# A latent-token backbone on one core: the down products of three stages as seven half products instead of eight

## The chip, the cores and the metric

The kernel runs on one core of a Trainium2 chip. The metric is the device time of one execution in microseconds (us): the median of several runs. Beside the runs one execution was profiled; its trace is what the rows below are from. The engines are TensorE (PE, with its weight loads as PEld), VectorE (DVE), ScalarE (ACT), GpSimd (POOL) and SyncE (SP, which here only issues DMAs). Each takes its instructions in order; they wait for each other by semaphores.

## What is computed

The program is a two-layer backbone on 1024 tokens of width 1024 (float32), with 256 context tokens. Layer 0 has a mixer of neighbourhood attention and a recurrent group, then a SwiGLU FFN; layer 1 has a short gated convolution, then a SwiGLU FFN. The change lies in the last three of these four parts:

```
def swiglu(h, w_gu, w_down):
    gt, up = jnp.split(h @ w_gu, 2, axis=-1)
    return (jax.nn.silu(gt) * up) @ w_down

def short_conv_mixer(h, w_in, w_conv, w_out):
    bg, cg, xv = jnp.split(h @ w_in, 3, axis=-1)
    return (bg * dwconv(cg * xv, w_conv, SC_PAD)) @ w_out

# layer 0:  h = h + g1 * mixer(...);  h = h + g2 * swiglu(modulate(rmsnorm(h)), ...)
# layer 1:  h = h + g1 * short_conv_mixer(...);  h = h + g2 * swiglu(...)
# output:   rmsnorm(h, final_g)
```

The hidden width of the FFN is 2816 (22 tiles of 128), of the short convolution 1024 (8 tiles). The gates, shifts and scales (g1, g2, ...) are the mod vectors, the product of a conditioning vector with mod_w, 6 x 1024 per layer.

## The kernel before

Features lie on the 128 partitions, tokens on the free axis; h is 8 tiles of 128 x 1024 in SBUF. Every product is done in three matmuls on a high and a low part of each operand: w_hi x_hi, w_lo x_hi, w_hi x_lo (the helper product, lines 1099 to 1104, so all matmuls have the lines L1102 to L1104). The high part is a cast by ScalarE, the low part a subtraction by GpSimd or VectorE.

The last three parts are three stages, F0 (FFN of layer 0), S (short convolution), F1 (FFN of layer 1). Each has a first phase of pairs and a down phase.

A pair makes two feature tiles of the input projection for all tokens (gate and up of the FFN; in S two of three are "sum" pairs, which make cg and xv and then the taps of the convolution, and every third is a "gated" pair, which makes bg for two tiles). A pair is 7 half products instead of 8, by Winograd's form of Strassen's scheme: the token axis and the contraction are halved, sums of the quadrants of weights and tokens are multiplied, and sums of the products give the result. So each pair has four weight sums by VectorE (weight_sum, L2086), seven operands cast by ScalarE (operand_high, L1602) and subtracted by GpSimd (operand_low, L1054), and VectorE's sums of products (pair_sums, L2240), 84 matmuls in all. The operands of pair p+1 are made while pair p is multiplied. The gated result z, two halves of 512 tokens, is stored to DRAM (store_z, L776, from silu_g or conv_t). F0 and F1 have 22 pairs, S has 12. The first four pairs of a stage have their products 0 and 3 done ahead, in first_products (L1418).

The down phase multiplies z with w_down (w_out in S) in rounds of two hidden tiles: 11, 4 and 11 rounds. A round loads two z tiles and two weight tiles (load_round, L838; 512 KB each), ScalarE casts (down_high, L1656), GpSimd makes the low parts (down_low, L1070), and PE runs 16 groups, 8 feature tiles by 2 token halves, each of 6 matmuls (down_group, L1484). After each group VectorE adds gate x result to h (update, L2052). The last two rounds are taken together, so that each group is done once with 12 matmuls, and the norm of the next stage begins beside its second half. Three sets of operand tiles (a, b, c) rotate.

In F0's down phase VectorE also makes the mod vectors of layer 1: 48 units, each a load of 512 KB (load_mod_f, L787) and a multiply-add of 1024 elements (mod_unit, L2060), summed over partitions by PE every 8 units. At the end of F1 the 8 token tiles of h are transposed by PE, squared, scaled and stored, four of them beside the last groups (fin_products, L1533).

The order is written out by hand on each engine. SP issues nearly all loads and stores in one queue, in program order; a wait of SP holds back every later transfer. In a pair its order is: store the first half of z, load one weight tile for the next pair, store the second half, load the other (products_loads, L792 to L825).

## Time and profile before

| | us |
|---|---|
| median of 3 runs | 2291.04 |
| lowest, highest run | 2290.49, 2293.44 |
| profiled execution, its span | 2288.6 |
| TensorE busy | 2234.8 |
| VectorE busy | 1484.0 |
| GpSimd busy | 1143.8 |
| ScalarE busy | 840.3 |

The page gives the profiled execution's span alone, from its first to its last instruction; the runs lie some us above it for what lies around the program. Matmuls overlap in the trace (each lasts 390 ns or so and the next starts earlier), so the busy time of PE tells that it is working, and the distance of starts tells what one costs. The granted clock is at its full level (0.9 or more in each slice).

### The profile page before, as it was taken

The numbers are of one execution on the slowest core, as the hardware profiler recorded it, in microseconds if no ns is written. First come the engines' busy times: TensorE is split into PE (matmuls) and PEld (weight loads), VectorE is DVE, ScalarE is ACT, GpSimd is POOL, SyncE is SP. The second block draws the span as 40 slices with busy tenths as digits, with TensorE's granted clock in tenths as the row PEclk, the third lists the DMA queues.
The fourth block names the chain that finished last, engine by engine and source line by source line (L and its number), as shares of the span: only waits on it lengthen the run. The fifth ranks groups of instructions, "written<-read, shape, count | busy, mean of one in ns | idle before, by whom it ended". The sixth has DMA issues, their size and how long they took to land.

```text
span 2288.6 us, 27308 instructions
## 1 busy us (share of the span) xinstructions
PE 2234.8 (98%) x10246; PEld 1822.6 (80%) x10246; DVE 1484.0 (65%) x1897; ACT 840.3 (37%) x1396; POOL 1143.8 (50%) x726
## 2 busy tenths in 40 slices
PE   8999999999899999999999999999899999999998
PEld 3788887878688888888888778888688888888886
DVE  5677856854876555558777987665965555555553
ACT  4555546853523332331213522233533333332212
POOL 3323304788455555565434345574365555564340
PEclk9999999999999999999999999999999999999999
DMA  9756568734132222257662122260132222242321
GB/s 332 223 159 175 159 177 205 163 131 134 42 101 83 83 83 83 83 192 258 207 208 78 51 74 74 74 215 2 60 102 90 83 83 83 84 151 90 111 83 74
DMA packets 296942, 282.95 MB, mean 124 GB/s; under 512 B 64783, under 2 KB 242155, under 8 KB 296299
## 3 DMA queue, kind: packets, MB, share of 16 engines
q1 hardware_dynamic: 258747, 257.61, 36.4%
q10 hardware_dynamic: 37488, 21.50, 3.3%
q0 software_dynamic: 576, 2.10, 0.2%
q8 instruction: 82, 1.34, 0.2%
q14 instruction: 49, 0.40, 0.1%
HBM read 226.36 MB, written 57.16 MB: 124 GB/s over the span
## 4 chain that ended last, share of the span: by engine, by line
PE 85%; DVE 6%; DMA 2%; ACT 2%; issue 2%; POOL 1%; SPq 0%; ACTq 0%; DVEq 0%; POOLq 0%
PE bank L1102 27%; PE bank L1104 26%; PE bank L1103 26%; PE bank L1191 1%; DMA q_spill<-qk_raw 1%; PE bank L1332 1%; DVE act_lo L2138 1%; DVE act_hi L2138 1%; PE bank L1357 1%; PE bank L1145 1%; PE bank L1316 1%; PE bank L1358 0%; DVE probs L2519 0%; DVE x_rms L2130 0%; DMA k_lo<-k_spill 0%
## 5 line engine op out<-in xcount | busy, mean ns | idle before, releaser
L2057 DVE SCALAR_TENSOR_TENSOR h<-bank,mods,h 128x512 f32<-128x512 f32 x384 | 287.4, 750 | 260.4 <-PE bank L1104 255.3
L1063 POOL TENSOR_TENSOR slot_lo<-pair_raw,slot_hi 128x512 fp32r<-128x512 f32 x112 | 169.8, 1516 | 288.0 <-ACT slot_hi L1621 288.0
L1063 POOL TENSOR_TENSOR slot_lo<-t_sum,slot_hi 128x512 fp32r<-128x512 f32 x109 | 164.5, 1531 | 153.4 <-ACT slot_hi L1621 153.4
L1063 POOL TENSOR_TENSOR slot<-pair_raw,slot 128x512 fp32r<-128x512 f32 x144 | 232.2, 1634 | 16.0 <-ACT slot L1621 16.0
L2218 DVE TENSOR_TENSOR bank<-bank,p 128x512 f32<-128x512 f32 x53 | 37.0, 698 | 288.3 <-PE bank L1104 288.2
L1102 PE MATMUL bank<-act_lo,slot_hi 128*128 128x512 f32 x436 | 171.1, 392 | 6.6 <-DVE act_lo L2138 5.9
L1621 ACT CAST slot_hi<-pair_raw 128x512 fp32r<-128x512 f32 x112 | 69.0, 616 | 294.4 <-DMA pair_raw<-in_ffn_w_gu 243.6
L1102 PE MATMUL bank<-a,slot_hi 128*128 128x512 f32 x436 | 171.5, 393 | 2.8 <-ACT p L1630 0.9
L1104 PE MATMUL bank<-a,slot_hi 128*128 128x512 f32 x436 | 170.5, 391 | 0.0
L1103 PE MATMUL bank<-act_lo,slot_lo 128*128 128x512 f32 x436 | 169.9, 390 | 0.0
L1104 PE MATMUL bank<-act_lo,slot_hi 128*128 128x512 f32 x436 | 169.9, 390 | 0.0
L1103 PE MATMUL bank<-a,slot_lo 128*128 128x512 f32 x436 | 169.7, 389 | 0.0
L1102 PE MATMUL bank<-act_hi,w_hi 128*128 128x512 f32 x368 | 146.7, 399 | 3.3 <-DVE proj_lo L2392 2.7
L1103 PE MATMUL bank<-act_hi,w_lo 128*128 128x512 f32 x376 | 148.0, 394 | 0.0
L1074 POOL TENSOR_TENSOR act_lo<-low_f,act_lo 128x512 fp32r<-128x512 f32 x80 | 102.3, 1315 | 85.3 <-ACT act_lo L1661 85.3
L1103 PE MATMUL bank<-act_hi,slot 128*128 128x512 f32 x364 | 141.9, 390 | 0.0
L1104 PE MATMUL bank<-act_hi,slot 128*128 128x512 f32 x364 | 141.8, 390 | 0.0
L1102 PE MATMUL bank<-act_hi,slot 128*128 128x512 f32 x364 | 141.7, 389 | 0.0
L1621 ACT CAST slot_hi<-t_sum 128x512 fp32r<-128x512 f32 x109 | 67.8, 622 | 160.6 <-PE bank L1104 103.3
L1102 PE MATMUL bank<-act_lo 128*128 128x512 f32 x320 | 125.8, 393 | 0.0
L1104 PE MATMUL bank<-act_lo 128*128 128x512 f32 x320 | 125.1, 391 | 0.0
L1103 PE MATMUL bank<-act_lo 128*128 128x512 f32 x320 | 124.6, 389 | 0.0
(329 smaller groups left out, 5975.0 us busy)
## 6 DMA issues: line engine op xcount, KB each, us to landing
pair_raw<-in_ffn_w_gu SPq DMA_DIRECT2D x88, 512.0 KB, 4.6
mod_in_f<-in_mod_w SPq DMA_DIRECT2D x48, 512.0 KB, 3.7
z_spill<-silu_g SPq DMA_DIRECT2D x88, 256.0 KB, 2.6
mod_in_p<-in_mod_w SPq DMA_DIRECT2D x32, 512.0 KB, 4.5
pair_raw<-in_o_w_in SPq DMA_DIRECT2D x24, 512.0 KB, 3.8
raw<-in_e_w_in SPq DMA_DIRECT2D x20, 512.0 KB, 4.4
low_f<-z_spill SPq DMA_DIRECT2D x40, 256.0 KB, 5.1
a_f<-z_spill SPq DMA_DIRECT2D x18, 512.0 KB, 6.2
```

Source lines behind the costliest of these rows:

```text
L1063: nc.gpsimd.tensor_tensor(low, from_, high, ALU.subtract).then_inc(s_wlo, 1)
L1074: nc.gpsimd.tensor_tensor(lo, full, hi, ALU.subtract).then_inc(s_l2, 1)
L1102: pe.matmul(dst, w_hi, x_hi, start=first, stop=False)
L1103: pe.matmul(dst, w_lo, x_hi, start=False, stop=False)
L1104: return pe.matmul(dst, w_hi, x_lo, start=False, stop=last)
L1145: mm = pe.matmul(bank[:, b, m:m + 1], acc[:, m * P:(m + 1) * P], ones[:, 0:1], start=True, stop=True)
L1191: mm = pe.matmul(bank[0:2, 4 + 2 * c + a, :], cond[:, k, :], mod_ring[:, u % 8, a * HALF:(a + 1) * HALF], start=(k == 0), stop=(k == FT - 1))
L1316: pe.matmul(out_, q, kh[:, part], start=True, stop=False)
L1621: nc.scalar.copy(slot(st, n, p)[0], from_).then_inc(s_whi, 1)
L2057: V.scalar_tensor_tensor(out=dst, in0=bank[:, b, :], scalar=mods[:, gate, m:m + 1], in1=dst, op0=ALU.mult, op1=ALU.add).then_inc(s_hup, 1)
L2138: V.tensor_tensor(lo, LOW_F[n][k], hi, ALU.subtract).then_inc(s_ld, 1)
L2218: V.tensor_tensor(to, bank[:, x_bank(p), :], p1_at(p), ALU.add).then_inc(s_made, 1)
```

## The change

The down phase is now done by the same scheme as the pairs. For hidden tiles 2r and 2r+1 the weights are quartered (two tiles by two halves of the output features) and z likewise (two tiles by two token halves). Seven products, each over all pairs kp of hidden tiles, are accumulated in PSUM one after the other: a product of 11 (or 4) steps, a step being one 128 x 512 weight piece by one 128 x 512 token piece, 4 output tiles of 3 matmuls. DOWN gives for each product its weight operand, its token operand, the four banks, and whether the banks start fresh or go on; UPDATES gives the quadrants of h to which VectorE adds the banks when the product is complete. So some products pass into several quadrants of h, and a bank that is carried on serves the next product too. The last four steps of a stage are done output tile by output tile.

The token sums T1 to T4 are made by VectorE in the pairs, from the two z tiles in one buffer zt (z_sum), and stored beside B11, B21, B22: 7 pieces per pair of tiles. The weight sums S1 to S4 are made in the pairs too: SP loads the four quarters of two weight tiles (load_w) a pair ahead, GpSimd makes S1 and S3, VectorE S2 and S4, in place, and SP stores the four sums (store_w), which stand behind the next pair's loads in the queue. The working space for this, and for the mod units, is that of h: h is stored to DRAM in pair 1 of each stage (put_h_aside) and fetched back in the last but one (bring_h_back). The mod units move from F0's down phase into the pairs 4 to 19 of F0 (32 units) and 2 to 9 of S (16), two per pair, with their sum in SBUF where it was in PSUM; two buffers instead of four.

The down phase loads each step into one of 8 slots (load_step); ScalarE casts both pieces, GpSimd makes the low part of the weights, VectorE that of the tokens from the fifth step on. Norm, first operands and first half of the next stage are spread over the steps of the last products (down_step on ACT, DVE and POOL). In the final rows the upper features of tiles 4 to 7 are transposed and multiplied by the gain beside the last product, and the last rows are done by halves.

The core of the diff:

```
+B11, B21, B22, T1, T2, T3, T4 = range(7)
+S1, S3, S2, S4 = range(4)
+DOWN = (((0, 0), B11, XS, True), (S2, T2, YS, True), ((1, 0), B21, XS, False), (S3, T3, YS, False),
+        ((1, 1), T4, YS, False), (S1, T1, XS, True), (S4, B22, XS, False))
+UPDATES = (((0, 1), (1, 0), (1, 1)), ((0, 1),), ((0, 0),), ((1, 1),), ((1, 0),), ((1, 1),), ((0, 1),))
...
+def w_ops(st, p):
+    return [k for k in range(4 * KP[st]) if W_PAIR + k // 8 * 3 + k % 8 // 3 == p]
...
+def w_loads(st, p):
+    return [kp for kp in range(KP[st]) if W_PAIR + kp // 2 * 3 + kp % 2 - 1 == p]
...
+    def store_t(kp, c):
+        sp.wait_ge(*z_summed(kp, c))
+        store_z(c, kp, {T1: zt[:, 0, one], T2: p1[:, 1, :], T3: zt[:, 0, two], T4: zt[:, 1, one]}[c])
+    def store_w(st, k):
+        r, c = divmod(k, 4)
+        kp = KP0[st] + r
+        sp.wait_ge(*w_made(kp, c))
+        sp.dma_start(w_sums[c, r], w_part[:, kp % 2, W_PIECE[c], :]).then_inc(s_wst[kp % 2], 16)
+    def load_w(st, r):
+        kp = KP0[st] + r
+        if kp >= 2:
+            sp.wait_ge(s_wst[kp % 2], 64 * (kp // 2))
+        sp.wait_ge(s_hst, X_DONE + 16 * (st + 1))
+        for a in (0, 1):
+            for j in (0, 1):
+                sp.dma_start(w_part[:, kp % 2, 2 * a + j, :],
+                             weights_down(st)[(2 * r + j) * P:(2 * r + j + 1) * P, a * HALF:(a + 1) * HALF]).then_inc(s_wld[kp % 2], 16)
+    def put_h_aside(st):
+        sp.wait_ge(s_scal, 8 * (NORM[st] + 1 - N_F0) + FT)
+        sp.dma_start(h_spill, h[:, :, :]).then_inc(s_hst, 16)
+    def bring_h_back(st):
+        for j in (0, 1):
+            sp.wait_ge(s_wst[j], 64 * ((KP0[st] + KP[st] + 1 - j) // 2))
+        if st != F1:
+            sp.wait_ge(s_mfin, LT + (4 if st == F0 else MODS) + 1)
+        sp.dma_start(h[:, :, :], h_spill).then_inc(s_hld, 16)
+    def aside_work(st, p):
+        for k in w_ops(st, p):
+            store_w(st, k)
+        for r in w_loads(st, p):
+            load_w(st, r)
+        for u in mod_units(st, p + 1):
+            load_mod_f(u)
+        if p == PAIRS[st] - 2:
+            bring_h_back(st)
...
+    def load_step(st, i):
+        q, r = divmod(i, KP[st])
+        w, c, *_ = DOWN[q]
+        kp = KP0[st] + r
+        if i < RING:
+            sp.wait_ge(s_prod, product_at(st, (1, 1, 2, 2, 4, 5, 6, 6)[i], PAIRS[st] - 1) + 1)
         else:
+            sp.wait_ge(*step_done(st, i - RING))
+        landed = down_landed(st, i)[0]
+        if isinstance(w, tuple):
+            from_ = weights_down(st)[(2 * r + w[0]) * P:(2 * r + w[0] + 1) * P, w[1] * HALF:(w[1] + 1) * HALF]
+        else:
+            from_ = w_sums[w, r]
+        sp.dma_start(down_operand(i)[0][2], from_).then_inc(landed, 16)
+        sp.wait_ge(*stored(c, kp + 1))
+        sp.dma_start(down_operand(i)[1][2], z_parts[c, r]).then_inc(landed, 16)
...
+    def w_sum(st, k):
+        r, c = divmod(k, 4)
+        kp = KP0[st] + r
+        a11_, a12_, a21_, a22_ = (w_part[:, kp % 2, j, :] for j in range(4))
+        if c == S1:
+            pool.wait_ge(s_wld[kp % 2], 64 * (kp // 2 + 1))
+            ins = nc.gpsimd.tensor_tensor(a22_, a21_, a22_, ALU.add)
+        else:
+            ins = nc.gpsimd.tensor_tensor(a21_, a11_, a21_, ALU.subtract)
+        ins.then_inc(s_wsum, 1)
...
+    def bank_free(st, q, m):
+        if q == 0:
+            if m == 0:
+                pe.wait_ge(s_xfree, PAIR0[st] + PAIRS[st])
+            if m == 3 and st != F1:
+                pe.wait_ge(s_mset, LT + (4 if st == F0 else MODS))
+        elif q == 1:
+            if m == 0:
+                pe.wait_ge(*made(PAIR0[st] + PAIRS[st] - 1, C21))
+        else:
+            pe.wait_ge(*updated(st, {2: 0, 3: 1, 4: 3, 5: 2, 6: 5}[q], m))
+    def down_part(st, i, m):
+        q, r = divmod(i, KP[st])
+        banks, fresh = DOWN[q][2:]
+        if r == 0:
+            bank_free(st, q, m)
+        w, x = down_operand(i)
+        at_ = slice(m * P, (m + 1) * P)
+        end = r == KP[st] - 1
+        mm = product(bank[:, banks[m], :], (w[0][:, at_], w[1][:, at_]), x[0], x[1], fresh and r == 0, end, not fresh)
+        if end:
+            mm.then_inc(s_out, 1)
+        return mm
...
     def down_products(st):
+        for i in range(n - TAIL):
+            down_ready(st, i)
+            for m in range(4):
+                mm = down_part(st, i, m)
+            if i % KP[st] < KP[st] - 1:
+                mm.then_inc(s_step, 1)
+            down_joint(st, i)
+        for i in range(n - TAIL, n):
+            down_ready(st, i)
+        for m in range(4):
+            if st == F1 and m == 3:
+                fin_lower(4, (0, 1))
+                fin_lower(5, (0, 1))
+            for i in range(n - TAIL, n):
+                down_part(st, i, m)
...
+    def z_sum(kp, c):
+        a, b, c_, d, t2 = zt[:, 0, one], zt[:, 0, two], zt[:, 1, one], zt[:, 1, two], p1[:, 1, :]
+        if c == T1:
+            dve.wait_ge(*stored(B11, kp + 1))
+            ins = V.tensor_tensor(a, b, a, ALU.subtract)
+        elif c == T3:
+            dve.wait_ge(*z_summed(kp, T1))
+            ins = V.tensor_tensor(b, d, b, ALU.subtract)
+        elif c == T2:
+            if kp:
+                dve.wait_ge(*stored(T2, kp))
+            ins = V.tensor_tensor(t2, d, a, ALU.subtract)
+        else:
+            dve.wait_ge(*stored(B21, kp + 1))
+            dve.wait_ge(*z_summed(kp, T2))
+            ins = V.tensor_tensor(c_, c_, t2, ALU.subtract)
+        ins.then_inc(s_zsum, 1)
+    def w_sum(st, k):
+        r, c = divmod(k, 4)
+        kp = KP0[st] + r
+        a11_, a12_, _, a22_ = (w_part[:, kp % 2, j, :] for j in range(4))
+        if c == S2:
+            dve.wait_ge(*w_made(kp, S3))
+            ins = V.tensor_tensor(a11_, a22_, a11_, ALU.subtract)
+        else:
+            dve.wait_ge(*w_made(kp, S2))
+            ins = V.tensor_tensor(a12_, a12_, a11_, ALU.subtract)
+        ins.then_inc(s_wsum_d, 1)
+    def before_pair(st, p):
+        if st == S and p % 3 == 0 and p:
+            dve.wait_ge(s_z1, PAIR0[S] + p)
+            for c in (T1, T3, T2, T4):
+                z_sum(KP0[S] + p // 3 - 1, c)
+        if st != S and p % 2:
+            dve.wait_ge(s_z1, PAIR0[st] + p)
+            z_sum(KP0[st] + p // 2, T1)
+        if st != S and p % 2 == 0 and p:
+            for c in (T2, T4):
+                z_sum(KP0[st] + p // 2 - 1, c)
+        for k in w_ops(st, p):
+            if k % 4 in (S2, S4):
+                w_sum(st, k)
+        for u in mod_units(st, p):
             mod_unit(u)
+        for n in mods_summed(st, p - 1):
             mod_set(LT + n, MODS + n)
...
+    def down_low(st, i):
+        hi, lo, full = down_operand(i)[1]
+        dve.wait_ge(*down_high_at(st, i, 1))
+        V.tensor_tensor(lo, full, hi, ALU.subtract).then_inc(s_lz, 1)
...
+    def down_step(st, j):
+        k, nx = KP[st], st + 1
+        q, r = divmod(j, k)
+        n = NORM[nx] if st != F1 else None
+        if r == k - 1:
+            if q == 0:
+                dve.wait_ge(s_hld, X_DONE + 16 * (st + 1))
+            elif q != 2:
+                dve.wait_ge(*updated(st, {1: 0, 3: 1, 4: 0, 5: 3, 6: 1}[q], 3))
+            for m in range(4):
+                for to in UPDATES[q]:
+                    down_update(st, q, m, *to)
+                if st != F1 and q == 6 and m:
+                    add_squares(n + 1, 3 + m)
+            if st != F1 and q == 4:
+                for i in range(4, FT):
```

## Rows read from the trace of the kernel before

**Rows 1.** The page: the span, and busy us (share, instructions) of each engine.

```profile
span 2288.6 us, 27308 instructions
...
PE 2234.8 (98%) x10246; PEld 1822.6 (80%) x10246; DVE 1484.0 (65%) x1897; ACT 840.3 (37%) x1396; POOL 1143.8 (50%) x726
```

**Rows 2.** The chain that ended last, share of the span by engine.

```profile
PE 85%; DVE 6%; DMA 2%; ACT 2%; issue 2%; POOL 1%; SPq 0%; ACTq 0%; DVEq 0%; POOLq 0%
```

**Rows 3.** Stretches: length; busy PE, PEld, DVE, ACT, POOL; clock, DMA share, GB/s.

```profile
632.90:1013.80 380.90, 380.90 (x1675) 314.05 (x1674) 219.20 (x270) 116.06 (x200) 215.00 (x140) 1.00 0.29 89
...
1308.00:1368.00 60.00, 55.00 (x232) 42.65 (x232) 53.27 (x63) 14.73 (x22) 29.44 (x19) 1.00 0.26 80
...
1380.00:1437.30 57.30, 57.30 (x253) 47.26 (x252) 39.00 (x46) 16.06 (x27) 30.91 (x22) 1.00 0.24 74
...
1019.00:1240.00 221.00, 221.00 (x1022) 184.34 (x1021) 167.62 (x207) 48.47 (x66) 106.42 (x60) 1.00 0.61 210
...
2035.00:2253.00 218.00, 218.00 (x961) 180.01 (x960) 113.56 (x152) 41.14 (x54) 100.95 (x56) 1.00 0.27 96
```

**Rows 4.** PE in order of time (start, us): first and last of 55 matmuls.

```profile
999.70 0.39 PE L1104 MATMUL bank<-act_lo,slot_hi 128*128 128x512 f32 x1
...
1011.95 0.39 PE L1104 MATMUL bank<-a,slot 128*128 128x512 f32 x1
```

**Rows 5.** DVE in order of time, steady pairs of F0 (idle before, releaser).

```profile
890.33 0.70 DVE L2218 TENSOR_TENSOR bank<-bank,p 128x512 f32<-128x512 f32 x1 [7.37 <-PE bank L1104]
...
892.26 0.68 DVE L2098 TENSOR_TENSOR t_sum<-pair_raw 128x512 f32<-128x512 f32 x1
...
909.42 0.70 DVE L2218 TENSOR_TENSOR bank<-bank,p 128x512 f32<-128x512 f32 x1 [7.38 <-PE bank L1104]
...
914.07 1.85 DVE L2108 TENSOR_TENSOR pair_raw<-pair_raw 128x512 f32<-128x512 f32 x1
```

**Rows 6.** POOL in order of time, in the same pairs.

```profile
898.47 4.74 POOL L1063 TENSOR_TENSOR slot<-pair_raw,slot 128x512 fp32r<-128x512 f32 x3
909.14 1.29 POOL L1063 TENSOR_TENSOR slot_lo<-pair_raw,slot_hi 128x512 fp32r<-128x512 f32 x1 [5.94 <-ACT slot_hi L1621]
```

**Rows 7.** Groups by shape: count | busy, mean ns | idle before, releasers.

```profile
L2057 DVE SCALAR_TENSOR_TENSOR h<-bank,mods,h 128x512 f32<-128x512 f32 x384 | 287.4, 750 | 260.4 <-PE bank L1104 255.3
...
L1074 POOL TENSOR_TENSOR act_lo<-low_f,act_lo 128x512 fp32r<-128x512 f32 x80 | 102.3, 1315 | 85.3 <-ACT act_lo L1661 85.3
...
L2449 DVE SCALAR_TENSOR_TENSOR mod_acc_p<-mod_in_p,cond,mod_acc_p 128x1024 f32<-128x1024 f32 x28 | 49.5, 1768 | 2.6
L2070 DVE SCALAR_TENSOR_TENSOR bank<-mod_in_f,cond,bank 128x1024 f32<-128x1024 f32 x36 | 46.1, 1280 | 0.0
...
L1661 ACT CAST act_lo<-low_f 128x512 fp32r<-128x512 f32 x80 | 43.6, 617 | 121.9 <-DMA low_f<-in_ffn_w_down 94.1 <-DMA low_f<-in_o_w_out 22.2 <-DMA low_f<-z_spill 5.6
...
L1573 ACT ACTIVATE sq<-h 128x512 f32<-128x512 f32 x48 | 30.4, 642 | 100.3 <-DVE h L2057 100.3
...
L1583 ACT ACTIVATE a<-bank,mods 128x512 fp32r<-128x512 f32 x24 | 16.9, 705 | 0.0
```

**Rows 8.** DMA issues: count, KB each, median us from issue to landing.

```profile
pair_raw<-in_ffn_w_gu SPq DMA_DIRECT2D x88, 512.0 KB, 4.6
...
z_spill<-silu_g SPq DMA_DIRECT2D x88, 256.0 KB, 2.6
...
low_f<-z_spill SPq DMA_DIRECT2D x40, 256.0 KB, 5.1
...
h_spill<-h_in ACTq DMA_DIRECT2D x1, 4096.0 KB, 13.7
```

**Rows 9.** DVE in order of time, pairs of S.

```profile
1354.22 0.69 DVE L2098 TENSOR_TENSOR t_sum<-pair_raw 128x512 f32<-128x512 f32 x1 [3.49 <-DMA pair_raw<-in_o_w_in]
...
1388.83 0.70 DVE L2218 TENSOR_TENSOR bank<-bank,p 128x512 f32<-128x512 f32 x1 [4.54 <-PE bank L1104]
```

**Rows 10.** Waits of SP's queue: us in total, times, longest.

```profile
SPq L774 <- PE bank L1145: 20.0, 1, 20.0
```

More of the change, by code:

```diff
@@ new lines, in backbone @@
+        B11, B21, B22, T1, T2, T3, T4 = range(7)
[3 more added lines that the diff above has]
+        UPDATES = (((0, 1), (1, 0), (1, 1)), ((0, 1),), ((0, 0),), ((1, 1),), ((1, 0),), ((1, 1),), ((0, 1),))
+        UPDATED = tuple(4 * sum(len(u) for u in UPDATES[:q]) for q in range(8))
+        TAIL = 4
+        BOTH = 4
@@ new lines, in feature, with step_done, down_operand @@
+        def feature(n, i):
+            return (i + 4) % FT if n in (N_S + 1, N_F1 + 1) else i
+        def step_done(st, i):
+            q, r = divmod(i, KP[st])
+            if r == KP[st] - 1:
+                return out_done(st, q, 3)
+            return s_step, sum(6 * (KP[k] - 1) + KP[k] - TAIL for k in range(st)) + q * (KP[st] - 1) + r + 1
+        def down_operand(i):
+            s = i % RING
+            if s < 4:
+                return tuple((act_lo[:, k, one], act_lo[:, k, two], low_f[:, k, two]) for k in (2 * s, 2 * s + 1))
+            if s < 6:
+                return tuple((act_hi[:, k, two], act_hi[:, k + 1, two], x_rms[:, k + 1, two]) for k in (4 * s - 16, 4 * s - 14))
+            return tuple((a22[:, k, one], a22[:, k, two], a22_f[:, k, two]) for k in (2 * s - 12, 2 * s - 11))
@@ new lines, in down_landed, with down_high_at, down_low_at @@
+        def down_landed(st, i):
+            before = sum((steps_of(k) - i % RING + RING - 1) // RING for k in range(st))
+            return s_land[i % RING], MOD_DONE + 32 * (before + i // RING + 1)
+        def down_high_at(st, i, j):
+            return s_h2, 2 * sum(steps_of(k) for k in range(st)) + 2 * i + j + 1
+        def down_low_at(st, i, j):
+            if j == 1 and i >= BOTH:
+                return s_lz, sum(steps_of(k) - BOTH for k in range(st)) + i - BOTH + 1
+            return s_l2, sum(steps_of(k) + BOTH for k in range(st)) + (2 * i + j + 1 if i < BOTH else i + BOTH + 1)
@@ L1636, in silu_first @@
-                if p:
-                    act.wait_ge(s_zst[0], 16 * done)
-                nc.scalar.activation(silu_g[:, 0, :], bank[:, x_bank(p), :] if p else silu_g[:, 0, :], ACT.Silu).then_inc(s_xfree, 1)
+                if kp and p % 2 == 0:
+                    act.wait_ge(*stored(T1, kp))
+                    act.wait_ge(*z_summed(kp - 1, T2))
+                if kp and p % 2:
+                    act.wait_ge(*stored(T4, kp))
+                to = zt[:, p % 2, one]
+                nc.scalar.activation(to, bank[:, x_bank(p), :] if p else to, ACT.Silu).then_inc(s_xfree, 1)
@@ L2299, in pair_work @@
                         c = PAR["short_w"] + j * FT + tile
-                        steps.run(V.scalar_tensor_tensor(out=conv_t[:, tile % 2, :], in0=t_pad[:, j:j + SEQ], scalar=par[:, c:c + 1],
-                                                         in1=conv_t[:, tile % 2, :], op0=ALU.mult, op1=ALU.add))
-                else:
-                    V.tensor_tensor(conv_t[:, 0, two], first, conv_t[:, 0, two], ALU.mult).then_inc(s_z0, 1)
-                    V.tensor_tensor(conv_t[:, 1, two], c22, conv_t[:, 1, two], ALU.mult).then_inc(s_z1, 1)
@@ L2306, in mods_here @@
-            def mods_here(r, idx):
-                for u in mod_units(r, idx):
+                        steps.run(V.scalar_tensor_tensor(out=zt[:, tile % 2, :], in0=t_pad[:, j:j + SEQ], scalar=par[:, c:c + 1],
+                                                         in1=zt[:, tile % 2, :], op0=ALU.mult, op1=ALU.add))
+                else:
+                    V.tensor_tensor(zt[:, 0, two], first, zt[:, 0, two], ALU.mult).then_inc(s_z0, 1)
+                    V.tensor_tensor(zt[:, 1, two], c22, zt[:, 1, two], ALU.mult).then_inc(s_z1, 1)
```

815 lines of the change are left out of this document (430 added, 385 removed).

## The prediction

> **What bounds the kernel now.** I read the busy line of the page first: TensorE is busy 2234.8 of 2288.6 us, VectorE 65%, GpSimd 50%, ScalarE 37% [rows 1]. The reader is to see that only TensorE has no room. The chain of waits says the same: 85% of it is PE, 6% VectorE, 2% DMA [rows 2]. Then the table by stretches: in the steady pairs of the first FFN (632.9 to 1013.8) and in the down products (1019 to 1240, 2035 to 2253) PE is busy for the whole stretch; in the first pairs of the short-convolution stage (1308 to 1368) it isn't: 232 matmuls in 60 us [rows 3]. A busy PE is pipelined, so the price of one matmul is its pitch, not its 390 ns: from 999.70 to 1011.95 lie 54 pitches, 12.25 / 54 = 0.2268 us [rows 4]. At that pitch 380.9 us hold 1679 matmuls and the row has 1675: full. A pair (7 products of 12) takes 84 x 0.2268 = 19.05 us, which is the distance of VectorE's first sum of a pair to the next, 909.42 against 890.33: 19.09 us [rows 5]. Matmuls taken out of such a stretch take their pitch out of the span, as long as nothing else becomes late.
>
> **The change, part by part.**
>
> *Fewer matmuls.* Down products before: 26 rounds (11, 4, 11), each 16 groups of 6, 2496 matmuls. After: 7 half products over 26 pairs of hidden tiles, 182 steps of 12, 2184. 312 fewer at 0.2268 us: -70.8 us. The matmuls that are left have the same shape. The mod totals and the norms keep their matmuls.
>
> *The down steps.* A step is 12 x 0.2268 = 2.72 us. It needs 0.524 MB (two loads of 256 KB): 193 GB/s, where the down rounds of the last stage moved 96 GB/s and those of the first, with the mod units beside them, 210 GB/s at a DMA share of 0.61 without a wait of PE [rows 3]. Eight slots: a slot is freed at the end of step i-8, so 7 steps, 19 us, lie before its next use. In them: landing 5.1 us for such a load in a burst [rows 8], two casts by ScalarE of 0.617, one low part by GpSimd of 1.315 [rows 7], together 7.7 us. The cover is 11 us, so I cost it at nothing; what it costs when gone is the third rival. Per step ScalarE needs 1.23, GpSimd 1.3, VectorE one low part of about 1, each under 2.72. The largest knot is the end of the first half product: 12 updates of 0.75 us [rows 7] are 9.0 us, 3.3 steps, and VectorE's low parts run 4 steps ahead: 0 to 1 us per stage, nothing taken. The updates fall from 368 to 108 in the three stages (the first 16, of the mixer, stay), so VectorE gains room here.
>
> *The sums in the pairs.* This is where the change adds. Per pair, VectorE gets: token-half sums, 2 (first and last stage) or 1.33 (middle); its half of the weight sums, 8 per three pairs of which 4, 1.33; and the mod units, moved from the down stage, 2 per pair in pairs 4 to 19 of the first stage and 2 to 9 of the middle. GpSimd gets 1.33 sums. A short VectorE sum takes 0.68 us alone and 1.85 when a GpSimd operation runs beside it (rows at 892.26 and 914.07) [rows 5]; a mod unit 1.28 to 1.77 [rows 7]. A weight sum of GpSimd is 1.3 to 1.6, like its other operations [rows 6].
> First stage: VectorE is busy 219.2 / 380.9 x 19.09 = 10.99 us per pair [rows 3]. Added from below 3.33 x 0.68 + 2 x 1.28 = 4.8, from above 3.33 x 1.85 + 2 x 1.77 = 9.7. The place is the wait of 7.38 us before a pair's first sum [rows 5]. GpSimd ends its run of three about 1.2 us into that wait (898.47 + 4.74) [rows 6] and with two sums more 4 us into it, so I price the short sums half and half at 1.25: 3.33 x 1.25 + 2 x 1.4 = 7.0, inside 7.38. If the first sum is late, PE notices after 4.0 us: it has two more products (5.44 us) before the one that needs the second sum, which takes 1.4. So 0 to 3 us; from above 10.99 + 9.7 - 19.09 = 1.6 us for each of 16 pairs, 26 us. I take 2.
> Middle stage: 39.0 / 3 = 13.0 us of 19.1 per pair [rows 3], since the taps sit there too; after a tap pair the wait is only 4.54 us [rows 9]. Added from below 2.67 x 0.68 + 2.56 = 4.4, total 17.4; from above 2.67 x 1.85 + 3.54 = 8.5, total 21.5, 2.4 us over in each of 8 pairs, 19 us. Besides, the sum T4 of a triple waits until B21 is stored, and that store is issued behind both loads of the next pair (4.6 us to land, then 2.6 [rows 8]): VectorE stands in order behind it, with all sums of the next pair, and this one wait alone may eat the 4.0 us of PE's patience. I take 1 us per pair, 8 us. A gain stands against it: SP's wait of 20.0 us for the last mod total before the stage's first load goes [rows 10], and of the 60 us from 1308 on, 7.4 us of pitches are lost now, partly to late weights (3.49 us at 1354) [rows 9]; so the bounds are -3 and +19.
> Last stage: 10.99 + 3.33 x 1.85 = 17.2 us at most, under 19.09: nothing.
>
> *Queues.* On SP, behind each new wait stand the next pair's loads. In a steady pair it would be done about 11 us after the pair's start (z sums, weight sums, mod units in this order), 7 us before its next first wait, the store of the gated half. GpSimd's sum waits for weights loaded a pair ahead; should they come 4 us late, its low parts for the next pair still have 6 us. The traffic of a first-stage pair is 1 MB weights, 0.9 z, 1.3 weight sums, 1 mods: 4.4 MB in 19.09 us, 231 GB/s, by the same row near 0.67 of the engines [rows 3]. Putting h aside (4 MB, 13.7 us [rows 8]) lies in pair 1, fetching it back in the last two pairs with 30 us before the first update: nothing.
>
> *Seams.* First to middle: the norm of the first token half is done steps earlier, the chain after the last product (update, square, add, sum) is as long as before: 0. Middle to last: only 5 steps (13.6 us) lie between that norm and the stage's end, and ScalarE needs 8 features x 2 x 0.70 and 4 squares x 0.64, 13.8 us [rows 7], starting some us after the norm; VectorE's last updates stand behind them. +3 us (0 to 8). Also in the middle stage, step 7 needs the T2 of the last triple, whose sum, store and load fill the 19 us before it: +1 (0 to 4). The end after the last product has a shorter row step and one more copy on ScalarE: 0, plus or minus 2.
>
> **Sum.** 2288.6 - 70.8 + 2 + 8 + 3 + 1 = 2231.8 us of span. The page gives no total for the profiled execution; the median of the runs, 2291.04, is 2.4 above its span. Forecast 2234 us, its own range 2226 to 2246.
>
> *A rule weighed.* The row: a VectorE sum from two SBUF inputs takes 0.68 or, when it meets a GpSimd operation of 1.29, up to 1.85 [rows 5, 6]. The Trainium skill ("SBUF — State Buffer", Who interferes with whom) says more: a VectorE instruction with two SBUF inputs and a GpSimd one that reads SBUF exclude each other, the second blocks fully until the first ends. 0.68 + 1.17 agrees with that. By the rule every added sum also costs GpSimd, and nothing overlaps; that is the second rival below.
>
> **Rivals.**
> *All hidden.* VectorE waits 7.4 us in each pair of the first and last stage and the late start of the middle stage heals. 2288.6 - 70.8 - 3 + 2.4 = 2217, or 2220 without the healing. For it: the waits in rows 5; against: the 4.54 us in rows 9.
> *VectorE and GpSimd set the pair.* Every added sum finds GpSimd working: +26 and +19 as worked out, +4 of the seams: 2288.6 - 70.8 + 49 + 2.4 = 2269. For it: 1.85 us rows stand already in the trace. Against: half of the wait has GpSimd idle.
> *Loads set the down steps (slower than before).* Place: the 182 steps; price: what a step waits for its 0.524 MB. At 150 GB/s a step is 3.50 us, 0.77 x 182 = 141 us more: 2288.6 - 70.8 + 141 + 2.4 = 2361. It decides from 70.8 / 182 = 0.39 us per step, 3.11 us, 169 GB/s downward. For it: 193 GB/s are asked without a pause and a 256 KB load in a burst takes 5.1 us [rows 8]. Against: 210 GB/s ran over 221 us at 0.61 of the engines [rows 3].
>
> **Numbers.** Forecast 0.60, all hidden 0.18, VectorE and GpSimd 0.16, loads 0.06. What a measurement of this kernel can tell from no change is about 0.2%, 4.6 us. Range 2218 to 2262: the forecast's cases, most of the hidden ones and the nearer part of the second rival, some 0.8. Faster 0.92, same 0.02, slower 0.06.
>
> **What would show it.** Right: 312 matmuls fewer, pitch 0.227 in the down steps, steady pairs of the first and last stage still 19.1 us apart, those of the middle near 20, PE busy throughout. The second rival shows as pairs of 20.5 us or more in which PE waits for VectorE's second sum or GpSimd's low part; the third as PE waiting in down steps for low parts and ScalarE for loads. Wrong altogether: pairs of the last stage, without mod units, over 19.5 us.

## The result, and the profile after

The changed kernel takes 2305.28 us (median of 6 runs, 2297.57 to 2307.13) against 2292.24 beside it: ratio 1.0051, 95% interval 1.0037 to 1.0065, slower by half a per cent. The forecast was 2234. The profiled execution is the shortest of the six (2297.57), so stretches below add up to some 8 us less than the medians.

The page of the changed kernel answers [rows 1, 2]: span, busy times, and the chain that ended last (its shares add to 36% here, to 98% before; read them by proportion).

```profile
span 2295.8 us, 27820 instructions
PE 2184.8 (95%) x9934; PEld 1766.2 (77%) x9934; DVE 1758.6 (77%) x1967; ACT 938.5 (41%) x1620; POOL 1275.4 (56%) x828
...
PE 12%; POOL 9%; DMA 6%; DVE 5%; ACT 2%; issue 1%; SPq 1%; ACTq 0%; DVEq 0%
```

The 312 matmuls are gone, but PE is idle for 111 us where it was idle for 54, and the chain, 85% PE before, now runs as much over GpSimd and DMA as over PE. Stretches of the changed kernel, to set beside [rows 3] (columns as there): steady pairs of F0 (p4 to p21), early pairs of S (p1 to p4), steady pairs of F1, down products of F1.

```profile
692.04:1025.30 333.26, 330.32 (x1479) 272.15 (x1478) 307.96 (x311) 97.88 (x170) 219.85 (x139) 1.00 0.64 225
...
1304.86:1363.28 58.42, 48.02 (x193) 37.48 (x192) 52.72 (x56) 12.96 (x20) 31.08 (x19) 0.91 0.52 174
...
1728.54:2059.02 330.48, 325.93 (x1424) 266.13 (x1423) 279.09 (x276) 97.87 (x170) 219.48 (x139) 1.00 0.53 181
...
2070.00:2275.00 205.00, 204.57 (x923) 168.88 (x923) 127.65 (x121) 92.95 (x171) 110.03 (x78) 1.00 0.62 201
```

The down products keep PE full. The pairs of F1, which carry no mod work, don't. The table divides each span at VectorE's first sum of a pair (p0, p4, ...), in us; p0 to p4 are called the early pairs, the later ones steady. "Pitch" is before less the fewer matmuls (29.9, 10.9, 29.9 us), with the six mod totals, 1.7 us each, moved from the down products of F0 into the pairs. E1, E5, E9 and E13 are experiments below.

| stretch | before | pitch | changed | E1 | E5 | E9 | E13 |
|---|---|---|---|---|---|---|---|
| F0 p0 to p4 | 61.3 | 61.3 | 71.0 | 70.3 | 70.1 | 70.1 | 65.5 |
| F0 p4 to p21 | 324.8 | 331.5 | 333.3 | 328.9 | 328.9 | 328.9 | 331.2 |
| F0 p21 to S p0 | 298.0 | 258.0 | 260.2 | 259.0 | 259.0 | 259.1 | 260.7 |
| S p0 to p4 | 65.9 | 65.9 | 77.8 | 78.3 | 79.2 | 75.8 | 71.2 |
| S p4 to p11 | 134.7 | 138.1 | 148.6 | 150.8 | 151.3 | 141.9 | 138.3 |
| S p11 to F1 p0 | 134.6 | 123.7 | 150.1 | 150.1 | 139.9 | 138.2 | 139.9 |
| F1 p0 to p4 | 61.3 | 61.3 | 66.5 | 68.1 | 67.7 | 67.8 | 66.0 |
| F1 p4 to p21 | 324.8 | 324.8 | 330.5 | 322.5 | 322.1 | 322.1 | 324.8 |
| F1 p21 to the end | 264.5 | 234.6 | 236.7 | 235.3 | 235.3 | 235.3 | 235.3 |

Against "pitch" the changed kernel loses 26.8 us in the three sets of early pairs, 18.0 in the steady ones, 26.4 from S into F1, 4.4 in the other down products and 2.2 ahead of them.

### The profile page after: what moved, and what is told of

The parts are those of the page before. It is cut to its first block and busy times, and to the rows that moved or that the text cites. A ratio compares the mean times of both kernels' runs of the same rounds, so it can differ in the third digit from the quotient of the medians.

```text
span 2295.8 us, 27820 instructions
## 1 busy us (share of the span) xinstructions
PE 2184.8 (95%) x9934; PEld 1766.2 (77%) x9934; DVE 1758.6 (77%) x1967; ACT 938.5 (41%) x1620; POOL 1275.4 (56%) x828
## 5 line engine op out<-in xcount | busy, mean ns | idle before, releaser
L1157 POOL TENSOR_TENSOR slot_lo<-pair_raw,slot_hi 128x512 fp32r<-128x512 f32 x112 | 174.8, 1561 | 296.6 <-ACT slot_hi L1751 296.6
L1157 POOL TENSOR_TENSOR slot<-pair_raw,slot 128x512 fp32r<-128x512 f32 x144 | 245.0, 1714 | 10.7 <-ACT slot L1751 10.7
L1179 POOL TENSOR_TENSOR act_lo<-low_f,act_lo 128x512 fp32r<-128x512 f32 x108 | 155.8, 1454 | 121.9 <-ACT act_lo L1793 121.8
L1228 PE MATMUL bank<-a,slot_hi 128*128 128x512 f32 x436 | 176.1, 404 | 24.5 <-ACT zt L1769 7.5
L1230 PE MATMUL bank<-a,slot_hi 128*128 128x512 f32 x436 | 171.7, 394 | 0.0
L1793 ACT CAST act_lo<-low_f 128x512 fp32r<-128x512 f32 x192 | 109.7, 621 | 143.7 <-DMA low_f<-z_parts 143.6
L1228 PE MATMUL bank<-act_lo 128*128 128x512 f32 x384 | 151.7, 395 | 16.6 <-DVE h L2244 10.6
L1230 PE MATMUL bank<-act_lo 128*128 128x512 f32 x384 | 150.5, 392 | 0.0
L1229 PE MATMUL bank<-act_lo 128*128 128x512 f32 x384 | 150.2, 391 | 0.0
L1229 PE MATMUL bank<-act_hi,slot 128*128 128x512 f32 x364 | 141.9, 390 | 0.0
L1751 ACT CAST slot<-pair_raw 128x512 fp32r<-128x512 f32 x144 | 85.7, 620 | 125.0 <-DVE pair_raw L2296 65.4
L2555 DVE TENSOR_TENSOR act_lo<-low_f,act_lo 128x512 fp32r<-128x512 f32 x84 | 103.7, 1256 | 37.4 <-ACT act_lo L1793 37.4
```

Of the source, the lines that this page charges most:

```text
L1157: nc.gpsimd.tensor_tensor(low, from_, high, ALU.subtract).then_inc(s_wlo, 1)
L1179: nc.gpsimd.tensor_tensor(lo, full, hi, ALU.subtract).then_inc(s_l2, 1)
L1228: pe.matmul(dst, w_hi, x_hi, start=first, stop=False, skip_group_check=resumed)
L1229: pe.matmul(dst, w_lo, x_hi, start=False, stop=False, skip_group_check=resumed)
L1230: return pe.matmul(dst, w_hi, x_lo, start=False, stop=last, skip_group_check=resumed)
L1751: nc.scalar.copy(slot(st, n, p)[0], from_).then_inc(s_whi, 1)
```

## The experiments

Theories at the start. *Loop:* GpSimd's low part of operand 6 frees the raw weights, the next pair's load follows, then ScalarE's cast, then GpSimd's low parts; a sum put among these makes the circle longer. *VectorE:* its added sums stand ahead of a pair's first sum. *Traffic:* 1.3 MB per pair more slows every load.

The chain of the changed kernel through one steady pair of F1 (start, us, what) is the loop; L1170 and L1172 are the weight sums. (In the next pair it leaves the loop for VectorE's sums of the pair's weights.)

```profile
1843.56 5.54 DMA pair_raw<-in_ffn_w_gu
...
1849.17 0.63 ACT slot_hi L1751
...
1849.88 5.96 POOL slot_lo L1157 x4
1855.84 1.72 POOL slot L1157
1857.56 1.70 POOL w_part L1170
1859.26 1.72 POOL slot L1157
1860.98 1.70 POOL w_part L1172
1862.68 1.73 POOL slot L1157
...
1864.43 4.34 DMA pair_raw<-in_ffn_w_gu
```

**E1: GpSimd's weight sums behind operand 6.**

```diff
                     for n in operands(st, p):
                         operand_low(st, n, p)
-                        if n in (2, 4, 5) and ...:
-                            w_sum(st, sums[n // 2 - (n < 5)])
+                    for k in sums:
+                        if k % 4 in (S1, S3):
+                            w_sum(st, k)
```

> GpSimd's weight sums are moved behind its low part of operand 6, so they no longer stand between a pair's first low part and the one that frees the raw weights. Loop theory (low part of operand 6, load of the next pair, ScalarE's cast, the six low parts before the next operand 6: in the steady pairs of the changed kernel this circle is longer than 19.09 us): the distance of pairs 4 to 21 falls from 19.44 to 19.1 us in the last stage (-5.7 us), from 19.6 to 19.5 in the first (-1.8), and some 3 to 5 us come back in the middle stage: 2293 us against 2305. VectorE theory (the added sums of VectorE in front of a pair's first sum are what makes the pairs late) and traffic theory (the weight parts and sums slow every load): 2305, within 3.

2285.53 us, ratio to before 0.9972 (0.9961 to 0.9983): the same work in another place is 20 us faster. GpSimd in order of time (start, us, idle before and its releaser), first the changed kernel, then E1:

```profile
1849.88 1.29 POOL L1157 TENSOR_TENSOR slot_lo<-pair_raw,slot_hi 128x512 fp32r<-128x512 f32 x1 [6.34 <-ACT slot_hi L1751]
...
1869.54 1.29 POOL L1157 TENSOR_TENSOR slot_lo<-pair_raw,slot_hi 128x512 fp32r<-128x512 f32 x1 [5.14 <-ACT slot_hi L1751]
```

```profile
1859.05 1.29 POOL L1157 TENSOR_TENSOR slot_lo<-pair_raw,slot_hi 128x512 fp32r<-128x512 f32 x1 [2.99 <-ACT slot_hi L1752]
1862.28 3.08 POOL L1157 TENSOR_TENSOR slot_lo<-t_sum,slot_hi 128x512 fp32r<-128x512 f32 x2 [1.94 <-ACT slot_hi L1752]
...
1867.02 4.73 POOL L1157 TENSOR_TENSOR slot<-pair_raw,slot 128x512 fp32r<-128x512 f32 x3
...
1891.03 1.73 POOL L1170 TENSOR_TENSOR w_part<-w_part 128x512 f32<-128x512 f32 x1
1892.73 1.28 POOL L1172 TENSOR_TENSOR w_part<-w_part 128x512 f32<-128x512 f32 x1
```

In the steady pairs of F1 of the changed kernel GpSimd's round, from a pair's first low part to the next pair's, has two sums in two pairs of three: 14.1 to 14.5 us of GpSimd, then 5.1 to 6.9 of load and cast, 19.6 to 21.4 in all. Without sums it is 11.1 and 6.3 to 7.1, 17.4 to 18.3. The mean is 19.4, the distance of the pairs. In E1 the sums lie in the time of the load. ScalarE's casts then wait 14 times for PE last, that is for a free operand slot: the loads are back ahead of PE (waits from 1640 to 2060; the changed kernel has there 157.2 us for the load and 7.8, 3 times, for PE):

```profile
ACT slot_hi L1752 <- DMA pair_raw<-in_ffn_w_gu: 124.3, 17, 7.9
ACT slot_hi L1752 <- PE bank L1231: 50.6, 14, 9.8
```

PE is busy for all but 0.04 us of E1's steady pairs of F1:

```profile
1727.29:2049.81 322.52, 322.48 (x1418) 265.86 (x1417) 243.47 (x276) 99.11 (x170) 216.05 (x139) 1.00 0.54 184
```

The loop theory holds for the steady pairs; the early ones and S stay. The table shows 10.7 us of the 19.8: where the longer runs of the changed kernel lost the rest no profile shows.

**E2 to E4: sums and their traffic taken out of the changed kernel.**

```diff
# E2, each of VectorE's four token sums
-    ins = V.tensor_tensor(a, b, a, ALU.subtract)
+    ins = V.tensor_tensor(a[:, 0:1], b[:, 0:1], a[:, 0:1], ALU.subtract)
# E3, each of the four weight sums
-    ins = nc.gpsimd.tensor_tensor(a22_, a21_, a22_, ALU.add)
+    ins = nc.gpsimd.tensor_tensor(a22_[:, 0:1], a21_[:, 0:1], a22_[:, 0:1], ALU.add)
# E4, on top of E3; the loads of the weight parts likewise, and the down steps load plain weights, as many bytes
-    sp.dma_start(w_sums[c, r], w_part[:, kp % 2, W_PIECE[c], :])
+    sp.dma_start(w_sums[c, r][:, 0:8], w_part[:, kp % 2, W_PIECE[c], 0:8])
...
```

> VectorE's four token-half sums of a pair of hidden tiles are made on one column instead of 512; their stores and all waits stay (the sums are left out of the computation). VectorE theory: pairs 0 to 4 of each stage, 13.6 us apart, have no room for them, so these give back most of 9.7, 11.8 and 5.2 us, and the middle stage's later pairs half of 10.5: 2305 - 28 = 2277 us. Loop theory: only the early pairs, where GpSimd has no sums yet, may move; the steady ones stay at 19.44 and 19.6: 2295. Traffic theory: 2305, within 3.

> All four weight sums, GpSimd's and VectorE's, are made on one column; their loads, stores and waits stay (the sums are left out of the computation). Loop theory: as with GpSimd's sums moved, about 2293 or some us lower, since VectorE's two also go: steady pairs of the last stage 19.09 us. VectorE theory: steady pairs give back half of their 18 us, 2296. Traffic theory: 2305, within 3. Early pairs (0 to 4) stay as they are in all theories, since the weight sums begin with pair 4.

> As the kernel with all weight sums on one column, and besides the loads of the weight parts and the stores of the sums carry 8 columns instead of 512; the down steps load plain weights in place of the sums, the same bytes (the sums are left out of the computation). What it differs from that kernel by is the traffic of 1.3 MB per pair alone. Traffic theory: 15 us or more faster than that kernel, pairs 4 to 21 at 19.1 us in both outer stages. Loop and VectorE theories: the same as that kernel within 4 us, but for the landing times in the pairs (4.4 to 5.0 us), which fall.

E2: 2294.20 us (1.0003, 0.9992 to 1.0014), 11 less than the changed kernel and 17 more than the VectorE theory said; early pairs 67.8, 77.3, 65.1, together 5 us less; the two profiles are only 1 us apart, and where the rest of the 11 lies neither shows. E3: 2274.15 (0.9919, 0.9905 to 0.9934), F1's steady pairs 19.1 us each; 11 below E1, of it 9 in S (75.7 and 144.1 us, 7 less than in the changed kernel). E4: 2271.51 (0.9903, 0.9885 to 0.9922), 2.6 below E3 with overlapping intervals. So the weight sums' traffic (54 of the 141 MB that the change adds) costs nothing clear of noise, and not the 15 us of the traffic theory; the weight sums' own time is some 7 of the 22 us that S loses, the token sums' time 5 us in the early pairs and nothing that a profile shows elsewhere. E2 left the waits that stand before the token sums: these are next.

**E5, E6: from S into F1.** The chain of the changed kernel there, on PE's longest idle time:

```profile
1550.82 5.31 DMA slot_f<-in_ffn_w_gu
1556.77 1.04 ACT act_hi L1793 x2
...
1560.97 3.17 DVE a L2555 x2
1564.23 2.71 DVE h L2244 x4
1566.95 1.59 DVE act_lo L2555
1568.54 1.44 DVE sumsq L2210
...
1574.94 1.75 DVE sumsq L2213
...
1578.29 0.75 DVE h L2244
1579.17 0.76 PE bank L1228
```

A first operand of F1 lands, only then come ScalarE's casts for the down steps, VectorE's low parts and squares behind them, the updates of h, and PE. ScalarE's row in order of time, and PE's longest waits from 1500 to 1665 (us in total, times, longest):

```profile
1556.14 0.62 ACT L1751 CAST slot_hi<-slot_lo_f 128x512 fp32r<-128x512 f32 x1 [11.03 <-DMA slot_f<-in_ffn_w_gu]
```

```profile
PE bank L1228 <- DVE h L2244: 14.2, 2, 8.7
PE bank L1228 <- POOL act_lo L1179: 3.2, 1, 3.2
```

```diff
# E5, on top of E1; GpSimd's low parts of them likewise, from 15 on in place of k + 4
-                if k + 2 <= j < k + 9:
-                    operand_high(nx, *FIRST[j - k - 2])
+                at_ = 13 if st == S else k + 2
+                if at_ <= j < at_ + 7:
+                    operand_high(nx, *FIRST[j - at_])
# E6, on top of E5
+                back = 1 if st == S and i == 7 else 0
+                sp.wait_ge(*stored(c, kp + 1 - back))
+                sp.dma_start(down_operand(i)[1][2], z_parts[c, r - back])
```

> On top of the kernel with GpSimd's sums behind operand 6 (2285.5 us). In the middle stage's down products ScalarE's casts of the last stage's first operands stand at steps 6 to 12, and the first of them waits until all seven loads have landed, of which SyncE issues the last only when step 8 has ended; here the casts stand at steps 13 to 19 and GpSimd's low parts of them at 15 to 21; the loads stay where they are. Cast theory: ScalarE's wait of 10.9 us goes, the casts and squares behind it come on time, VectorE reaches the third updates earlier and TensorE's wait of 8.7 us for them goes: from pair 11 of the middle stage to pair 0 of the last 138 us instead of 150.1, 2274 us. Traffic theory (the burst of loads at 347 GB/s sets these steps, whoever casts): 2285, within 3. T2 theory (the load of step 7 waits for the stored T2 of the last triple and holds up SyncE's queue): 2285, within 3.

> As the kernel with the first casts later, and step 7 of the middle stage loads the T2 of the triple before, which was stored long ago (so the last triple's T2 is left out of the computation). T2 theory: SyncE's wait of 3.5 us goes, the loads of steps 8 to 16 go out some 4 us earlier, and TensorE's waits of 1.6 and 3.2 us in steps 6 to 11 go: 4 to 8 us less than that kernel. Cast and traffic theories: the same as that kernel within 3 us, since the loads of a burst land at the rate of the engines anyhow.

E5: 2275.23 us (0.9923, 0.9908 to 0.9938), 10.3 below E1, all of it in this stretch. The wait of 8.7 us is gone; PE's waits for h in E5:

```profile
PE bank L1230 <- DVE h L2247: 5.5, 1, 5.5
```

E6: 2275.01 (0.9923, 0.9906 to 0.9940), no difference: T2 costs nothing. The cast theory holds; ScalarE's casts and GpSimd's low parts of them were moved together.

**E7: the copy of h.**

```diff
# on top of E1
-                sp.dma_start(h_spill, h[:, :, :]).then_inc(s_hst, 16)
+                sp.dma_start(h_spill[:, :, 0:8], h[:, :, 0:8]).then_inc(s_hst, 16)
```

> On top of the kernel with GpSimd's sums behind operand 6, h is put aside in 8 of 1024 columns instead of whole (4 MB less traffic in pair 1 of each stage; what comes back is an old h, so the residual is left out of the computation). Traffic theory of the early pairs (the 4 MB stand in the queues before the loads of pairs 3 and 4, which then land 2.5 and 3.6 us late): pairs 0 to 4 come back from 70.3, 78.3 and 68.1 us by some 5 us each, 2285.5 - 15 = 2270. Queue theory (SyncE issues these loads late, behind the waits of the stores of the gated halves and token sums): within 3 us of 2285.

2284.50 us (0.9965, 0.9952 to 0.9978), early pairs 69.9, 78.8 and 68.3: 4 MB beside the early pairs cost nothing that these times show (1.0 us, within the interval).

**E8: last updates ahead of the squares.**

```diff
# on top of E5; ScalarE's four squares likewise, behind its first halves and not between them
                     for i in range(4):
                         scale(n, 2 + i, 2 + i)
-                        add_squares(n + 1, i)
...
                         for to in UPDATES[q]:
                             down_update(st, q, m, *to)
+                        if st == S and q == 6:
+                            add_squares(n + 1, m)
```

> As the kernel with the first casts later, and at the end of the middle stage VectorE makes the seven scales of the first token half without its four adds of squares between them; the adds follow between the last updates. Seam theory: TensorE waits 5.5 us at the first product of the last stage because VectorE's last updates stand behind four waits of 1.85 us for ScalarE's squares: 5 us less than that kernel. Rival: the norm of the second token half comes 3 us later instead, and the last stage's first pairs lose what was won: the same within 2 us.

2272.96 us (0.9911, 0.9897 to 0.9926): 2.3 below E5, within its interval, and the stretch 139.5 against 139.9. PE's wait for h there is gone, but one of 3.6 us for the first half's sum of squares came up in its place (0.4 in E5). That is nearer to the rival.

**E9 to E12: where VectorE's sums stand.** In the changed kernel T4 waits for the store of B21, and the whole next pair waits behind T4. A triple is two sum pairs and the gated pair of S. VectorE, then PE, at the border of the first two triples:

```profile
1339.26 0.69 DVE L2511 TENSOR_TENSOR zt<-zt,p 128x512 f32<-128x512 f32 x1 [4.52 <-DMA z_parts<-zt]
1339.87 3.67 DVE L2258 SCALAR_TENSOR_TENSOR mod_acc_f<-mod_in_f,cond,mod_acc_f 128x1024 f32<-128x1024 f32 x2
1343.46 0.69 DVE L2402 TENSOR_TENSOR bank<-bank,p 128x512 f32<-128x512 f32 x1
...
1344.80 0.79 PE L1228 MATMUL bank<-a,slot 128*128 128x512 f32 x1 [8.04 <-DVE p L2406]
```

```diff
# E9, on top of E8: S, before_pair
-                    for c in (T1, T3, T2, T4):
+                    for c in (T1, T3):
                         z_sum(KP0[S] + p // 3 - 1, c)
# S, end of a triple's first pair, ahead of the taps
+                    if p and p % 3 == 0:
+                        for c in (T2, T4):
+                            z_sum(KP0[S] + p // 3 - 1, c)
# S, SyncE's stores of T2 and T4, behind the pair's other work
-                        for c in (T1, T3, T2, T4):
+                        for c in (T1, T3):
                             store_t(KP0[S] + p // 3 - 1, c)
...
+                        for c in (T2, T4):
+                            store_t(KP0[S] + p // 3 - 1, c)
# E10: F0 and F1, taken out of before_pair, T2 behind the pair's first weight sums, and
# at the end of pair_sums (E11: the same for p <= 2 alone)
+                if st != S:
+                    z_sum(*((KP0[st] + p // 2, T1) if p % 2 else (KP0[st] + p // 2 - 1, T4)))
# E12, on top of E11: VectorE's weight sums in S, out of before_pair, behind pair_sums
+                    if st == S:
+                        own_w_sums(st, p)
```

> On top of the kernel with the updates before the squares (2273.0 us). In the middle stage VectorE makes T2 and T4 of a triple at the end of the next triple's first pair, not ahead of all its sums, and SyncE stores them behind that pair's other work. Store theory (T4 waits up to 6 us until B21 is stored, and VectorE with all sums of the pair stands behind it): the three distances at the triples' borders, 22.4, 24.9 and 25.2 us, fall to 20 or 21, together 10 to 13 us: 2261. Busy theory (VectorE has no room in the middle stage's pairs, wherever its sums stand): the time goes to other pairs, 2273 within 4.

> As the kernel with T2 and T4 later in the middle stage, and in the outer stages T1 stands behind a pair's sums, T2 behind its first weight sums and T4 behind its sums, where all three stood ahead of the pair's first sum. Store theory: in pairs 0 to 2, 10 to 15 us apart, VectorE has no wait to hide them in; distances 17.4 and 13.5 us fall towards the 15.1 and 10.5 of the kernel before, 4 to 5 us per outer stage: 8 to 10 us less than that kernel. Busy theory: the sums cost the same wherever they stand in a pair that VectorE fills; within 3 us of it.

> On top of the kernel with T2 and T4 later in the middle stage alone (2261.9 us): in pairs 1 and 2 of the outer stages only, where VectorE has no wait of its own, T1, T2 and T4 stand behind the pair's sums as in the last kernel; from pair 3 on they stand ahead of the pair again. Store theory: the distances 15.2 and 11.7 us of the last kernel stay (17.4 and 13.5 otherwise), pairs 3 and later are as in the kernel of 2261.9 us: 2254 to 2258 us. The loss of 86 us of the last kernel came from pairs of 20 to 26 us, in which ScalarE's gate waits for the moved sums and SyncE's queue for their stores; if T1 in pair 1 and T2, T4 in pair 2 alone do the same to pair 3, the time stays at 2262.

> As that kernel, and in the middle stage VectorE's two weight sums of a pair stand behind the pair's token sums, not ahead of them, where VectorE waits up to 2.5 us for GpSimd's S3 (which stands behind operand 6 now). In-order theory: the distances of 24.7 and 24.4 us from pair 3 to 4 and 6 to 7 fall by 2.5 to 4 us each, 5 to 8 us in all: 2250. Busy theory (VectorE is full in these pairs): the same within 2 us.

E9: 2261.92 us (0.9872, 0.9857 to 0.9887), 11 below E8; the store theory holds. VectorE's waits for B21's store at the three borders were, in E8 (us in total, times, longest):

```profile
DVE zt L2513 <- DMA z_parts<-zt: 11.5, 3, 4.2
```

In E9 they are gone, the three borders fell from 22.4, 24.9 and 25.2 us to 16.2, 19.2 and 19.0 (the pairs after two of them take over 3 more), and 12 us came back in S. SyncE's stores moved together with the sums; no run moves one without the other. This is the fastest version that leaves nothing out, 1.3% under the kernel before.

E10: 2347.82 us (1.0245, 1.0228 to 1.0262), 86 us more where 8 to 10 less were expected. Pairs 1 and 2 came as said (15.2 and 11.7 us), but the steady pairs of F0 take 17 to 26, together 52 us more than in E9, and those of F1 16 more; each outer stage takes 11 more after pair 21, where PE waits 9 us for ScalarE's work on the last gate. SyncE's waits in the steady pairs of F0, then ScalarE's longest:

```profile
SPq L837 <- DVE zt L2512: 116.5, 8, 15.2
...
SPq L834 <- POOL slot L1160: 8.2, 11, 1.8
...
ACT slot_hi L1756 <- DMA pair_raw<-in_ffn_w_gu: 170.7, 16, 12.7
```

The store of T1 now waits in SyncE's queue up to 15.2 us for VectorE, with the weight loads behind it. For the loads' buffer, which GpSimd frees, SyncE waits 8.2 us where it waited 71.6 in E9: it now comes to the loads late, and ScalarE waits 170.7 us for them where it waited 107.5. E10's chain there goes from T1 over its store in SyncE's queue to the next weight load. No run moves these stores alone. E11: 2263.43 (0.9877, 0.9863 to 0.9892), no gain: pairs 1 and 2 of F0 are 4 us shorter, pair 3 is 2.6 longer, since VectorE now waits 4.4 us for that pair's weights. E12: 2266.13 (0.9891, 0.9875 to 0.9908): from pair 3 to 4 and 6 to 7 of S it is 22.6 and 22.9 us, 1 to 2 less, and their neighbours take it back, as the busy theory said.

**E13, E14: what is left.**

```diff
# E13: E9 with the edits of E2 and E3. E14, on top of it:
+                    w = slice(0, UNIT if k == FT - 1 else 1)
+                    ins = V.scalar_tensor_tensor(out=to[:, w], in0=from_[:, w], ...)
```

> The kernel of 2261.9 us (three moves) with all token-half sums and weight sums on one column; waits, loads and stores stay (the sums are left out of the computation). What is still above the forecast of 2234 us is either the added engine work in the pairs or the path between the middle stage's last pair and the last stage's first (138.2 us where 123.7 were expected). Work theory: pairs 0 to 4 come back from 70.1, 75.8 and 67.8 us to some 64, 70 and 62, pairs 4 to 11 of the middle stage from 141.9 to 138: 2262 - 20 = 2242. Seam theory: the pairs have little left to give, 2262 - 8 = 2254, and 138 us stay in that path in both.

> As that kernel, and six of the eight steps of each mod's sum on one column too (also left out of the computation). If VectorE's mods (1.3 to 1.8 us each, two per pair in 16 pairs of the first stage and 8 of the middle) are among what fills the pairs, the middle stage's pairs 4 to 11 come down by some 4 us more; in the first stage, where VectorE waited 7.4 us per pair, nothing. If not, the same within 2 us.

E13: 2253.68 us (0.9839, 0.9824 to 0.9853): the engine time of all sums is 8.2 us in E9, as the seam theory said. E14: 2250.91 (0.9824, 0.9808 to 0.9841), 2.8 less, with overlapping intervals; the early pairs of S give 3.6 us and pairs 4 to 11 take them back. F1's early pairs, which have no mods, are 1.9 us shorter too, so single stretches are not sure to 2 us. Against "pitch" E13 keeps 14.2 us in the early pairs and 16.2 from S into F1, where PE's waits are, among others:

```profile
PE bank L1233 <- POOL act_lo L1182: 4.7, 1, 4.7
PE bank L1253 <- DVE sumsq L2218: 4.0, 1, 4.0
PE bank L1260 <- DVE diag L2227: 2.2, 1, 2.2
```

The chain of E13 in F0's early pairs (start, us, what): the store of B11 after pair 0, the first sum of pair 1, a weight load.

```profile
633.73 2.06 DMA z_parts<-zt
...
635.99 0.70 DVE bank L2407
...
647.64 6.28 DMA pair_raw<-in_ffn_w_gu
```

T1 waits for that store, and VectorE's first sum of pair 1 stands behind T1: p0 to p1 takes 16.9 us in F0 and F1, against 15.1 before and 15.2 in E11, which moves T1. From there the chain goes round the loop.

## Why the prediction was wrong, step by step

*Fewer matmuls, -70.8:* right. The down products of F0 and F1 came down by 37.8 and 27.7 us where 40.0 (with the mod totals that moved into the pairs) and 29.9 are the pitch.

*The down steps, nothing; loads (third rival):* right in F0 and F1, 201 GB/s without a wait worth naming. In S not: the cover of 7 steps was counted for the loads of a step and not for what else stands in ScalarE's order.

*Pairs of F1, 0; of F0, 2:* wrong by 10.9 and 9.5 us, and here the prediction failed first. The failed step is "should they come 4 us late, its low parts for the next pair still have 6 us", by which GpSimd's added sums cost nothing. Those 6 us are the 5.94 of [rows 6], and their releaser is ScalarE's cast, which waits for the load that GpSimd's own last low part lets go. They are the way back of a circle, not room. The room was another wait of the same pair, shown here as GpSimd and ScalarE had it before the change, for an operand slot that PE frees:

```profile
912.82 2.56 POOL L1063 TENSOR_TENSOR slot_lo<-t_sum,slot_hi 128x512 fp32r<-128x512 f32 x2 [2.40 <-ACT slot_hi L1621]
...
912.12 0.62 ACT L1621 CAST slot_hi<-t_sum 128x512 fp32r<-128x512 f32 x1 [3.06 <-PE bank L1104]
```

The prediction put VectorE's 17.2 us and PE's 19.09 side by side and never added up the circle: 10.7 us of low parts, 5.8 of load and cast and these 2.4 fill the 18.9 us to the next round. Two sums of 1.7 us are more than 2.4. E1 shows it by moving the same two sums to the other side of operand 6: the steady pairs are then under the pitch, and what F1 and F0 still lose, 4.5 and 6.4 us, comes from the early pairs.

*Early pairs:* no term at all, but for the copy of h, which is nothing indeed (E7). They are closer together than the steady ones, and VectorE waits for their weights even before the change [rows 9]; 26.8 us lost. In E9 it is 25.1, and 10.9 of these are the sums' time (E13); F0 and F1 make some 2.5 us each good again by p21. The last 14.2 stay with sums of one column. Of these 1.8 us in each of F0 and F1 are T1's wait for the store of B11 (E13's chain; E11 takes them away, but pair 3 gives them back); no run separates the rest.

*Pairs of S, 8:* mechanism right, size wrong. The wait of T4 for B21's store was named and priced at about 1 us per pair; its three waits take 10.9 us, the three borders took 23 to 25 us, and E9 got 11 back. In all, the pairs of S lose 22.4 us where 8 were taken. The healing of -3 from SyncE's wait [rows 10] did not come.

*Seams, 3 and 1:* 26.4, and of these 16.2 stay open in E13. The norm's share was seen (5.5 us of PE's wait, which E8 turned into another); T2 costs nothing (E6). Not seen: ScalarE's casts of F1's first operands stand at steps k+2 on, with k = 4 in S and 11 in F0, and wait for all seven loads, the last issued when step 8 has ended. 10.3 us (E5).

*Rivals.* None held. The second (VectorE and GpSimd set the pair, 2269) had the place but not the reason: in F1 neither engine was full, only their order was wrong. "Slower" came from no single rival: it took the loop, the casts in S and T4's wait together. The sign named for "wrong altogether", pairs of F1 over 19.5 us, was the right place to look: their mean is 19.44, single ones 21.4.

Together, 2305.3 - 19.8 (E1) - 10.3 (E5) - 2.3 (E8) - 11.0 (E9) = 2261.9, and 2253.7 without the sums' time. The other 20 us over the forecast lie in the early pairs and from S into F1. The kernel before took 2290.5 to 2293.1 us beside these runs, so each term is good to some 2 us.

## What to carry to other kernels

Before an engine's idle time is taken as room, follow its releaser round: if it leads back to that engine's own last instruction, the idle time is the rest of a circle, and what is added goes ahead of or behind the instruction that starts the next round at quite different prices (20 us here). A step that is copied from a long stage to a short one must be counted again in steps: at k+2 of 28 steps it stood ahead of its own loads. And a sum that waits for a store belongs behind the work that others wait for, unless its own store stands in a queue ahead of loads (E9 against E10).
